# Another order of weighing, scores and ScalarE's copies in the attention stage of a hybrid encoder

## What is computed

```python
def one_block(args):                      # one block of 128 queries, all heads
    q_blk, blk = args
    q_pos = blk * SB_BLOCK + jnp.arange(SB_BLOCK)
    visible = key_pos[None, :] < q_pos[:, None]
    z = jnp.einsum('bhqd,bhkd->bhqk', q_blk, k) * scale
    log_beta = jax.nn.log_sigmoid(z)
    log_keep = jnp.where(visible, log_beta - z, 0.0)
    log_w = log_beta + lax.cumsum(log_keep, axis=3, reverse=True) - log_keep
    w = jnp.where(visible, jnp.exp(log_w), 0.0)
    return jnp.einsum('bhqk,bhkd->bhqd', w, v)
```

## Time and profile before

| | us |
|---|---|
| median of 3 runs | 3014.12 |
| the runs | 3014.01 to 3014.28 |
| the profiled execution | 3014.04 |
| its span | 3012.3 |
| attention stage in it, about | 1889 to 2169.5 |

### The profile page before, as it was taken

How to read it: one execution, slowest core, us unless ns; L and a number is a source line. 1 busy time by engine, 2 the same in 40 slices (tenths; PEclk the granted TensorE clock), 3 DMA queues, 4 the chain that set the end, 5 groups by cost and what they waited for, 6 DMA issues and landing times.

```text
span 3012.3 us, 47062 instructions
## 1 busy us (share of the span) xinstructions
PE 2963.1 (98%) x19124; PEld 2680.1 (89%) x19124; DVE 1502.0 (50%) x2161; ACT 854.8 (28%) x1523; POOL 447.4 (15%) x504
## 2 busy tenths in 40 slices
PE   8999989999999999999999999999999999999998
PEld 7999978888999999999999997788888888888887
DVE  6777437766534444334346443667643333333434
ACT  4211245555221111111113101666612111111112
POOL 3000145655210000000000001000021000001000
PEclk9999989999999999999999999999999999999999
DMA  4333322112111111111111325555111111111111
GB/s 122 94 92 97 108 63 69 58 59 63 48 57 49 42 42 42 56 46 44 49 42 60 138 93 161 144 115 115 39 43 56 56 43 47 49 49 46 45 42 70
DMA packets 201831, 207.31 MB, mean 69 GB/s; under 512 B 8379, under 2 KB 172364, under 8 KB 201692
## 3 DMA queue, kind: packets, MB, share of 16 engines
q1 hardware_dynamic: 191114, 167.05, 19.5%
q0 software_dynamic: 10368, 38.21, 3.7%
q10 hardware_dynamic: 210, 0.07, 0.0%
HBM read 162.87 MB, written 42.44 MB: 68 GB/s over the span
## 4 chain that ended last, share of the span: by engine, by line
PE 95%; ACT 2%; issue 1%; DVE 1%; DMA 0%; POOL 0%; SPq 0%; ACTq 0%; DVEq 0%; POOLq 0%
PE PS L1870 20%; PE PS L1871 20%; PE PS L1872 20%; PE PS L2301 5%; PE PS L2300 5%; PE PS L2299 5%; PE PS L2422 2%; PE PS L2406 2%; PE PS L2084 1%; PE PS L2064 1%; PE PS L2373 1%; PE PS L2372 1%; PE PS L2011 1%; PE PS L2121 1%; PE PS L2111 1%
## 5 line engine op out<-in xcount | busy, mean ns | idle before, releaser
L1870 PE MATMUL PS<-YH,WL 128*128 128x348 f32 (+1 forms) x3040 | 1039.9, 342 | 3.7 <-DVE WL L1278 2.3
L1871 PE MATMUL PS<-YL,WH 128*128 128x348 f32 (+1 forms) x3040 | 1039.1, 342 | 0.0
L1872 PE MATMUL PS<-YH,WH 128*128 128x348 f32 (+1 forms) x3040 | 1038.1, 341 | 0.0
L1870 PEld LDWEIGHTS PS<-YH,WL 128*128 128x128 f32 x3040 | 571.9, 188 | 44.7 <-issue 3.1
L1871 PEld LDWEIGHTS PS<-YL,WH 128*128 128x128 f32 x3040 | 571.7, 188 | 37.8 <-issue 0.8
L1872 PEld LDWEIGHTS PS<-YH,WH 128*128 128x128 f32 x3040 | 572.9, 188 | 35.7
L1695 DVE TENSOR_TENSOR hT<-PS,hT 128x346 f32<-128x346 f32 (+2 forms) x440 | 251.6, 586 | 178.5 <-PE PS L2301 178.4
L808 POOL TENSOR_TENSOR gact<-gact,rs 128x346 f32<-128x346 f32 (+2 forms) x110 | 118.7, 1079 | 1307.1 <-ACT gact L1120 1307.1
L2299 PE MATMUL PS<-AH,WL 128*128 128x346 f32 (+2 forms) x880 | 308.6, 351 | 1.1 <-DVE AL L1685 1.1
L2301 PE MATMUL PS<-AH,WH 128*128 128x346 f32 (+2 forms) x880 | 308.8, 351 | 0.0
L2300 PE MATMUL PS<-AL,WH 128*128 128x346 f32 (+2 forms) x880 | 308.8, 351 | 0.0
(11 more groups left out here) (286 smaller groups left out, 3708.1 us busy)
## 6 DMA issues: line engine op xcount, KB each, us to landing
raw<-in_ffn_w_gate_up SPq DMA_DIRECT2D x88, 512.0 KB, 3.8
raw<-in_ffn_w_down SPq DMA_DIRECT2D x44, 512.0 KB, 3.7
s_in<-obuf POOLq DMA_DIRECT2D x32, 520.0 KB, 4.4
raw<-in_gdn_w_in SPq DMA_DIRECT2D x32, 512.0 KB, 4.2
Xqk<-s_in SPq DMA_DIRECT2D x10, 832.0 KB, 5.9
raw<-in_w_kv SPq DMA_DIRECT2D x16, 512.0 KB, 3.9
gBc<-s_g SPq DMA_DIRECT2D x10, 416.0 KB, 4.4
Xv<-s_in SPq DMA_DIRECT2D x10, 416.0 KB, 3.5
```

The costliest lines, as they stand in the source:

```text
L1870: pe.matmul(PS[:, bank, 0:n], wl, xh, start=(k == 0), stop=False)
L1871: pe.matmul(PS[:, bank, 0:n], wh, xl, start=False, stop=False)
L1872: m = pe.matmul(PS[:, bank, 0:n], wh, xh, start=False, stop=(k == KT - 1))
```

## The change

In `slot(U)` the weighing of U-1 and turn 1 of U move in front of the scores of U+3. On ScalarE the copy of turn 1 moves in front of the sigmoid of U+3; the copy of turn 2 stays behind it. No instruction is added or removed, and none changes its size.

```diff
@@ ScalarE @@
                 parts = len(TURNS[UNITS[u][1]])
-                take_turned(unit, 0)
+                for g in range(min(parts, 2)):
+                    take_turned(unit, g)
                 if unit + 3 < PAIRS * NU:
                     kept(unit + 3)
-                for g in range(1, parts):
-                    take_turned(unit, g)
+                if parts > 2:
+                    take_turned(unit, 2)
@@ TensorE, slot(U) @@
                 turn(U, 0)
+                if U and (U - 1) % 4 > 1:
+                    weigh(U - 1)
+                if parts > 1:
+                    turn(U, 1)
                 if U + 3 < PAIRS * NU:
                     scores(U + 3)
-                if parts > 1:
-                    turn(U, 1)
-                if U and (U - 1) % 4 > 1:
-                    weigh(U - 1)
                 if parts > 2:
                     turn(U, 2)
```

## The result

| | before | changed |
|---|---|---|
| median, us | 3014.03 (6 runs) | 3025.35 (6 runs) |
| lowest to highest | 3010.64 to 3014.28 | 3023.96 to 3027.77 |
| ratio | | 1.0042, 95% interval 1.0032 to 1.0052 |

What follows compares the result with a forecast made beforehand. TensorE's work bounds the attention stage, with small waits for ScalarE on top. Losses of 0.8 + 3.6 + 1.9 + 2.2 + 0.7 + 0.9 = 10.1 us on 3014.0 gave 3024.1 us, range 3016 to 3030.

Steps and rivals of the forecast that it cites:

- slot-by-slot layout: Attention stage: a pair's instructions laid out in the new order from measured durations and lags; period from 35.04 to about 36.3 us.
- slots taken to be unchanged: Slots 5, 8, 9, 11, 12, 15 keep their lengths; with slots 14 and 1 losing 0.04 and 0.05, 0.7 us in all.

Runs made afterwards that it cites:

- the result's copy later: Changed kernel with the pair's result copy on ScalarE moved from slot 4 to 12, its VectorE subtraction from unit 7 to 14; 3028.48 us.
- TensorE's part only: Kernel before with only TensorE's new order; ScalarE keeps the sigmoid of U+3 ahead of the copy of turn 1; 3054.72 us, ratio 1.0137.

## What to carry to other kernels

When an engine A feeds an engine B and waits for it later, ask of every reordering on A what it does to B's longest job: here scores issued late left ScalarE idle for 2 to 3 us and then put a sigmoid of 1 us in front of a copy of 0.25 us that A needed at once. In this kernel long work on A belongs behind the instruction that gives B its long job, and the short copies ahead of it. A slot-by-slot layout from measured lengths gave the period of the changed kernel and of the nine other orders tried here, 34 to 41 us, to within about 0.4 us (for the result's copy later, by two errors that cancelled); what it misses are the small lags in slots taken to be unchanged, so these deserve the same care as the places that the change names.

## What the runs showed of the hardware

- The lag from one engine's end to TensorE's start was 0.05 us for a transpose behind ScalarE's copy, but 0.14 behind VectorE's scan and for scores behind a sigmoid. Why they differ was not tried.
- Back-to-back activations overlapped by 0.09 us (1975.07 + 0.80 = 1975.87, the next at 1975.78). The Trainium skill ("ScalarE: Activation LUTs", What ACT_TABLE_LOAD costs) gives about 93 ns; the trace agrees.
- One kernel's executions spread over nearly 5 us (3010.36 to 3015.17 in 19 runs of the kernel before). The granted clock of the stage's first microseconds was 0.57 in one trace of it and 1.00 in the other, behind a wait of the same length (1.49 and 1.48 us); that accounts for 1.1 us between these two.
- In the kernel with the result's copy later the clock went to its lower level (0.50 over 2179.3 to 2181.8) behind waits of 1.48 and 1.26 us that stood close together. In the steady pairs the granted clock stayed at 1.00 with waits of up to 1.0 us (TensorE's part only, at the weighing of unit 15).
